# Forgetting attention of a fused transformer pair: when the value chunks are split, which banks the values go to, and when the gated rows' products start

## The reference, cut to what matters

```
def fox_attention(u, w_in, b_f, q_norm_g, k_norm_g, w_out):
    proj = u @ w_in
    q, k, v, g, fl = jnp.split(proj, [D_MODEL, 2 * D_MODEL, 3 * D_MODEL, 4 * D_MODEL], axis=-1)
    ...
    log_f = jax.nn.log_sigmoid((fl + b_f).astype(jnp.float32))
    f_cum = jnp.cumsum(log_f, axis=1).transpose(0, 2, 1)
    ...
        s = s + f_cum[:, :, t0:t1, None] - f_cum[:, :, None, :t1]
    ...
    return (o * jax.nn.sigmoid(g)) @ w_out
```

## Time and profile before

| what | value |
|---|---|
| three timed runs | 2485.5, 2488.03, 2491.11 us (median 2488.03) |
| the profiled execution's own time | 2469.53 us |
| its span, first to last instruction | 2467.5 us |
| mean granted TensorE clock | 0.954 of full speed |
| PE busy | 2248.9 us (91%) |
| DVE busy | 1244.2 us (50%) |
| ACT busy | 781.6 us (32%) |
| POOL busy | 126.0 us (5%) |

### The profile page before, as it was taken

How to read it: one execution, slowest core, us unless ns; L and a number is a source line. 1 busy time by engine, 2 the same in 40 slices (tenths; PEclk the granted TensorE clock), 3 DMA queues, 4 the chain that set the end, 5 groups by cost and what they waited for, 6 DMA issues and landing times.

```text
span 2467.5 us, 27898 instructions
## 1 busy us (share of the span) xinstructions
PE 2248.9 (91%) x10800; PEld 1562.3 (63%) x10800; DVE 1244.2 (50%) x1835; ACT 781.6 (32%) x1367; POOL 126.0 (5%) x154
## 2 busy tenths in 40 slices
PE   5899996988979999699989999989878788999997
PEld 5533333876743333377667888867667666888886
DVE  5411115556641111478776455668828835633455
ACT  4211113355211111453333313343226633322321
POOL 1111110000011111000000000000000000000000
PEclk9999997999979999799899999999989989999999
DMA  7899977210679997631124244221100041322220
GB/s 278 330 357 385 403 297 274 94 52 1 265 307 366 383 394 294 261 146 69 69 77 171 103 154 154 97 92 69 51 18 1 1 154 60 120 86 102 103 77 35
DMA packets 90851, 416.22 MB, mean 169 GB/s; under 512 B 16600, under 2 KB 16960, under 8 KB 51408
## 3 DMA queue, kind: packets, MB, share of 16 engines
q1 hardware_dynamic: 71024, 373.26, 39.5%
q0 software_dynamic: 19696, 41.17, 4.6%
HBM read 516.34 MB, written 31.98 MB: 222 GB/s over the span
## 4 chain that ended last, share of the span: by engine, by line
PE 74%; DVE 16%; ACT 4%; DMA 3%; issue 2%; POOL 0%; DVEq 0%; ACTq 0%; POOLq 0%
PE psum L109 15%; PE psum L111 15%; PE psum L110 15%; PE psum L875 14%; PE psum L898 7%; DVE w_low L316 2%; PE psum L865 2%; DVE w_low L1039 1%; ACT w_high L292 1%; DVE rg_in L2390 1%; DMA rows<-in_rows 1%; PE psum L885 1%; DMA raw<-in_ada 1%; DVE residual_tmp L1964 1%; DVE bn L1972 1%
## 5 line engine op out<-in xcount | busy, mean ns | idle before, releaser
L316 DVE TENSOR_TENSOR w_low<-raw,w_high 128x2048 fp32r<-128x2048 f32 (+2 forms) x110 | 245.5, 2238 | 239.2 <-ACT w_high L292 226.1
L109 PE MATMUL psum<-x_high,w_high 128*128 128x512 f32 x848 | 349.1, 412 | 16.0 <-DVE x_low L1039 9.3
L110 PE MATMUL psum<-x_high,w_low 128*128 128x512 f32 x848 | 340.4, 401 | 0.0
L111 PE MATMUL psum<-x_low,w_high 128*128 128x512 f32 x848 | 338.2, 399 | 0.0
L292 ACT ACTIVATE w_high<-raw 128x2048 fp32r<-128x2048 f32 (+2 forms) x110 | 204.8, 1870 | 286.6 <-PE psum L111 268.9
L111 PE MATMUL psum<-w_low,mlp_high 128*128 128x512 f32 x512 | 201.8, 394 | 0.0
L109 PEld LDWEIGHTS psum<-x_high,w_high 128*128 128x128 f32 x848 | 161.1, 190 | 63.7 <-ACT u_tile L1827 6.9
L109 PE MATMUL psum<-w_high,mlp_high 128*128 128x512 f32 x512 | 199.6, 390 | 1.3 <-DVE mlp_low L1039 1.3
L110 PE MATMUL psum<-w_high,mlp_low 128*128 128x512 f32 x512 | 200.6, 392 | 0.0
L110 PEld LDWEIGHTS psum<-x_high,w_low 128*128 128x128 f32 x848 | 161.0, 190 | 43.6 <-issue 5.8
L111 PEld LDWEIGHTS psum<-x_low,w_high 128*128 128x128 f32 x848 | 161.3, 190 | 39.1 <-issue 0.3
(11 more groups left out here) (562 smaller groups left out, 3977.4 us busy)
## 6 DMA issues: line engine op xcount, KB each, us to landing
raw_in_x<-in_moe SPq DMA_DIRECT2D x72, 1024.0 KB
raw<-in_moe SPq DMA_DIRECT2D x72, 1024.0 KB
raw<-in_mlp SPq DMA_DIRECT2D x64, 1024.0 KB
raw_in_high<-in_moe SPq DMA_DIRECT2D x54, 1024.0 KB
raw_in_low<-in_moe SPq DMA_DIRECT2D x54, 1024.0 KB
raw<-in_ada SPq DMA_DIRECT2D x48, 1024.0 KB
raw_extra<-in_moe SPq DMA_DIRECT2D x36, 1024.0 KB
raw<-in_evin SPq DMA_DIRECT2D x10, 1024.0 KB
```

The source lines that it names most:

```text
L109: pe.matmul(out, ah, bh, start=first, stop=False)
L110: pe.matmul(out, al, bh, start=False, stop=False)
L111: return pe.matmul(out, ah, bl, start=False, stop=last)
L316: dve.tensor_tensor(wl[:, 0:w], k.RAW[k.RAW_AT[c]][:, 0:w], wh[:, 0:w].bitcast(F32), ALU.subtract).then_inc(*k.V.step("low", c))
```

## The change

It has two parts. In `fox_in`, the high part of c+10 is made ahead of the exponential, and that of c+11 right behind it; that of c+12 is made ahead of the copy of the first half's values. On DVE the low part of c+10 moves ahead of the log-sigmoid's second piece, and that of c+11 stands where c+10's stood. The second half of the values goes to banks 4 to 7, so PE no longer waits for ACT's copies but for the last reads of these banks. In `fox_out`, ACT makes the next chunk's high part before it waits for the tile's products; PE begins the rows' products when the low part of gated tile 3 is there, waits for each bank's sigmoid ahead of it, spreads the diagonal two row tiles later, and waits for gated tile 7 only ahead of `last_rows_end`.

```diff
@@ last_rows_tensor
         if half:
             pe.wait_ge(*k.after("gate row", s))
-        else:
-            gate_tensor(k, pe, s)
         for t in range(XT):
+            if half == 0:
+                pe.wait_ge(*k.after("gate sigmoid", DK - XT + t))
+            if half == 0 and t == 2:
+                gate_tensor(k, pe, s)
             mm = part_rows(k, pe, half, t, 0, 4 * half + t, ah, al, pair)
         mm.then_inc(*k.T.step("used", c + half))
+    if s == 2:
+        pe.wait_ge(*k.after("gated lo", DK - 1))
     last_rows_end(k, pe, s, c, ah, al)
@@ new
+def v_bank_free(k, half, t):
+
+    if half == 0:
+        return k.after("fox qk", FT - 4 + t)
+    return k.after("forget gates read") if t == 2 else k.after("fox qk", FT - 1)
@@ fox_in_tensor
                 if q == 0:
-                    pe.wait_ge(*(k.after("fox v", 0, t) if half else k.after("fox qk", FT - 4 + t)))
+                    pe.wait_ge(*v_bank_free(k, half, t))
                 for f in range(4):
                     w = slice(f * HALF, f * HALF + HALF)
-                    mm = products(pe, k.PS[:, t, :], k.XH[:, 4 * q + f, t * P:(t + 1) * P],
+                    mm = products(pe, k.PS[:, 4 * half + t, :], k.XH[:, 4 * q + f, t * P:(t + 1) * P],
@@ fox_in_scalar
-    split_high(k, act, c + 9)
+    split_high(k, act, c + 10)
     log_sigmoid_scalar(k, act, k.FL[:, 1, :], "fox")
-    split_high(k, act, c + 10)
+    split_high(k, act, c + 11)
...
     for half in range(2):
-        if half:
+        if half == 0:
             split_high(k, act, c + 12)
         act.wait_ge(*k.after("fox v done", half))
         for t in range(XT):
-            act.activation(k.FV[:, t, half * HALF:(half + 1) * HALF], k.PS[:, t, :], ACT.Copy).then_inc(*k.A.step("fox v", half, t))
+            act.activation(k.FV[:, t, half * HALF:(half + 1) * HALF], k.PS[:, 4 * half + t, :], ACT.Copy).then_inc(
+                *k.A.step("fox v", half, t))
@@ fox_in_vector
-    log_sigmoid_vector(k, dve, x, e, z, q, "fox")
+    V.mark("forget gates read")
+    log_sigmoid_start(k, dve, x, e, "fox")
     split_low(k, dve, c + 10)
+    log_sigmoid_end(k, dve, x, e, z, q, "fox")
+    split_low(k, dve, c + 11)
@@ fox_out_tensor
-    pe.wait_ge(*k.after("gated lo", DK - 1))
+    pe.wait_ge(*k.after("gated lo", DK // 2 - 1))
     last_rows_tensor(k, pe, 2, c + 4, k.OH, k.OL)
@@ fox_out_scalar
     for m in range(DK):
-        act.wait_ge(*k.after("fox g", m))
         if m % 2:
             split_high(k, act, c + m // 2 + LOOK)
+        act.wait_ge(*k.after("fox g", m))
@@ fox_out_vector
-    split_low(k, dve, c + 5)
     gate_row(k, dve, 2)
```

## The result

The changed kernel took 2444.49, 2449.71, 2457.66 and 2442.53 us (median 2447.1), the kernel before beside it 2486.77 at the median. The ratio is 0.987, with a 95% interval of 0.983 to 0.991: between 22 and 41 us less. The profiled execution took 2444.49 us, with a span of 2442.5; its forecast counterpart was 2442.2.

What follows compares the result with a forecast made beforehand. PE was taken as the bound, losing time only where it stands still and at the lowered clock behind. Three stops, 8.5 + 9.2 + 9.6 = 27.3 us, off the median 2488.03 gave 2460.7 us, range 2451 to 2471.

Steps and rivals of the forecast that it cites:

- forecast counterpart: Predicted time of the changed kernel's profiled execution: 2469.53 of the kernel before less 27.3, giving 2442.2 us.
- First and second stop: PE's waits among the value products for the low parts of c+10 and c+11, with clock loss: 8.5 and 9.2 us saved.
- The three margins: How early the low parts of c+10, c+11 and c+12 would be ready for PE: 6.3, 3.1 and 2.1 us.
- Forget chain takes over: Rival: c+12's low part comes late, so PE stops after 144 value products; 20.2 us saved, 2467.8; chance 0.06.
- Third stop: PE's wait in `fox_out` between the gate's products and the gated rows, for tile 7's low part: 9.6 us saved.
- the end of the bounds that I chose: Length assumed for spreading the diagonal in `fox_out`: 1.72 us rather than 3.78; the other end would leave 7.5 us.
- Third stop moves: Rival: the rows' second half waits for DVE's gate row, or the join does; all 9.6 us return, 2470.3; chance 0.04.
- Cycling over more banks keeps the lower clock: Rival: breaks between 12-product groups of values and rows lower the clock; at worst 58 us cost, about 2518; chance 0.02.
- The change doesn't do what it says: Rival: a wait, being a count on a whole engine, still stands for something late; time near 2488; chance 0.02.
- The sum: Total predicted saving over the three stops of PE: 8.5 + 9.2 + 9.6 = 27.3 us.
- all times there 17.7 earlier: Assumption that everything in `fox_out` starts 17.7 us earlier, ahead of the saving at the rows.
- The step from the profiled execution to the median: Took the 27.3 us from the runs' median, 2488.03, which lies 18.5 above the profiled execution: 2460.7 us.

Runs made afterwards that it cites:

- chain_14: Changed kernel with two extra small DVE operations (1.39 us) in the forget gate's chain ahead of c+12's low part; a single time, 2440.75 us.
- chain_34: Changed kernel with one extra DVE reciprocal (3.34 us) in the forget gate's chain; a single time, 2460.35 us.
- p2_only: Kernel before with only the change's lines in `fox_out` and `last_rows_tensor` (gate and rows), values as before; ratio 0.997.
- early_nowarm: Changed kernel with the attention's first parts made ahead of the copies of the values' second half, and without PE's first ten warming products; ratio 0.983.
- p1_only: Kernel before with only the change's lines in `fox_in` (early low parts, banks 4 to 7), gate and rows as before; ratio 0.990.
- early_parts: Changed kernel with the attention's first low parts, blanks and rounded parts made ahead of the copies of the values' second half; ratio 0.986.
- chain_101: Changed kernel with three extra DVE reciprocals (about 10.1 us) in the forget gate's chain; a single time, 2454.74 us.
- splits_only: Values' part of the change alone, with early low and high parts but both halves of the values left in banks 0 to 3; ratio 0.996.

## Why the prediction was right, and where it was off

- *First and second stop.* The forecast was 8.5 + 9.2 = 17.7; measured are 17.68, and neither came back elsewhere. The three margins were forecast as 6.3, 3.1 and 2.1 us and are 6.6, 3.3 and 2.3.
- *Forget chain takes over* (0.06). It doesn't, but its margin is real: chain_14 fits into it and chain_34 does not. It is the next thing to break if that chain grows.
- *Third stop.* The forecast was 9.6; measured are 9.74 with the gate's clock as before (p2_only). The spreading took 1.88 us, so the end of the bounds that I chose was the right one. ACT's reordering, to which I gave tile 7's earlier time, isn't needed for it.
- *Third stop moves* (0.04). DVE's gate row is done at 2018.9, and the second half starts near 2023; there is no wait. The margin is about 4 us where 2.2 were forecast, since the gate row begins 2.0 us behind the spreading's start and not 3.9, which the forecast took from the kernel before, at the lower clock.
- *Cycling over more banks keeps the lower clock* (0.02). The 192 products over eight banks ran at a granted clock of 1.00, as the window above shows. The rule of the Trainium skill (TensorE: Matmul & The Clock Gate, "A second HAM failure mode: psum-queue depth-cycling") does not show itself in this kernel.
- *The change doesn't do what it says* (0.02). Every wait is where the order put it.
- *The sum.* **The step that failed is "all times there 17.7 earlier" for `fox_out`.** It carried the first eleven gate products over at their price of before. They cost 2.1 us less, because the granted clock, which falls during PE's last waits in the attention in both kernels, is up again ahead of the gate now, and was not before; why is open (last section). So the sum is 29.6 (17.7 + 9.7 + 2.1), not 27.3. These 2.1 us are luck as far as the forecast goes: nothing in it asked for them, and early_nowarm, whose values run without a stop too, doesn't get them.
- *The time.* 2460.7 against 2447.1 is mostly not the sum. The step from the profiled execution to the median took one stretch of three runs as the level of before. The stretches ahead of the change vary by 25 us from one execution to the next, and the ratio's interval, 22 to 41 us, holds both 27.3 and 29.6. The range failed by the same step: its lower end took that median for the level, and added only 7 us for an execution that had already been seen 18.5 below it. The profiled counterpart, 2442.2, came out at 2444.49, 2.3 later: 5.0 by the later start, less 2.1 by the gate's clock, and less 0.6 by smaller differences. The 0.2% that was to be told from no change was too fine as well: with four runs the interval is 0.4% to either side.

## What to carry to other kernels

Where PE stops for late operands, look for the second wait behind the first before pricing a repair: here buffers and low parts each hid the other, one alone was worth nothing, the other half, and both together all of it. Work out by how much the next chain is early, and measure it by adding work of known length. And compare stretch by stretch when stages that nobody touched vary more than the change is worth.

## What was not expected of the hardware

What is changed among the values decides the clock at the gate, 147 us later. Eight kernels have a stop among their values (5.7 to 7.8 us, or 1.3 in chain_34), and all eight run the first ten or eleven gate products at 1.2 GHz. The five that have no stop there and start the attention with PE's warming products (the changed kernel twice, p1_only, chain_14, early_parts) all run them at 2.4 GHz. But early_nowarm has no stop among the values either, and it runs them at 1.2 GHz; so the stop by itself is not what counts.

In all fourteen profiles PE does the same work, with the same four waits, in the last 12 us or so ahead of the gate, and the granted clock falls during the longest of these waits (3.71 us). What differs is where in this wait it falls. The windows from the fall to the rise, the kernel before, the changed one and early_nowarm:

```profile
1969.56:1983.21 13.65, 9.82 (x28) 7.89 (x29) 2.80 (x6) 1.99 (x4) 0.00 (x0) 0.50 0.32 126
```
```profile
1957.52:1964.35 6.83, 4.00 (x13) 3.32 (x14) 2.48 (x6) 0.60 (x1) 0.00 (x0) 0.50 0.00 0
```
```profile
1943.91:1957.57 13.66, 9.57 (x27) 7.72 (x28) 3.06 (x6) 1.93 (x5) 0.00 (x0) 0.50 0.31 115
```

The gate starts at 1978.29, 1965.58 and 1952.89. So the clock falls 8.7, 8.1 and 9.0 us ahead of it, and rises 4.9 us behind its start, 1.2 us ahead of it, and 4.7 us behind its start. This holds without exception: in the five profiles with a fast gate the clock falls 7.7 to 8.1 us ahead of the gate and is up before it, in the nine others it falls 8.7 to 9.3 us ahead and is up 4.4 to 5.0 us behind its start. A shift of some tenths of a microsecond between PE's work and the fall of the clock thus goes with 2.1 us at the gate. A stop among the values shifts it, and so does leaving out the warming products. Whether the shift is the cause of the early or late rise, and by what rule, these runs don't show.

What a stop costs in clock isn't fixed either: 2.59 and 2.70 us in the kernel before, 1.82 and 2.28 behind the same two stops in p2_only, 1.66 behind a stop of 7.8 us in chain_101, 1.59 behind one of 7.07 in splits_only (52.90 - 44.24 - 7.07), next to nothing at once behind 1.34.
